# RWKV state stage: GroupNorm passes moved to ScalarE, zero blocks left out, and the block inverse computed in 64x64 quadrants

## What is computed

```python
def step(state, inp):
    rt, wt, kt, vt, kkt, at = inp
    sa = jnp.einsum('bhvk,bhk->bhv', state, -kkt)
    state = (state * wt[:, :, None, :]
             + sa[..., :, None] * (kkt * at)[..., None, :]
             + vt[..., :, None] * kt[..., None, :])
    yt = jnp.einsum('bhvk,bhk->bhv', state, rt)
    return state, yt
...
_, y = lax.scan(step, s0, xs)
...
mean = jnp.mean(y, axis=-1, keepdims=True)
var = jnp.mean(jnp.square(y - mean), axis=-1, keepdims=True)
y = ((y - mean) * lax.rsqrt(var + GN_EPS)).reshape(B, S, D_RWKV)
y = y * gn_g.astype(jnp.float32) + gn_b.astype(jnp.float32)
bonus = jnp.sum((r_h * k_h * r_k).astype(jnp.float32), axis=-1, keepdims=True) * v_h.astype(jnp.float32)
y = y + bonus.reshape(B, S, D_RWKV)
```

## Time and profile before

| | |
|---|---|
| median of 3 runs | 4568.9 us (4567.1 to 4570.67) |
| profiled execution | 4565.9 us, span of its instructions 4563.8 us |
| instructions | 68323 |
| mean granted clock of TensorE | 0.963 |
| TensorE busy | 4174.7 us, 91% of the span |
| VectorE busy | 2632.5 us, 58% |
| ScalarE busy | 1344.7 us, 29% |
| GpSimd busy | 633.4 us, 14% |

### The profile page before, as it was taken

One profiled execution on the slowest core, in us unless ns is written; L12 is line 12 of the kernel. 1 busy time (PEld: TensorE's weight loads), 2 busy tenths in 40 slices (PEclk: granted clock), 3 DMA queues, 4 the chain that ended last, 5 costly groups with the idle time before them and its releaser, 6 DMA issues. The chain is left out here.

```text
span 4563.8 us, 68323 instructions
## 1 busy us (share of the span) xinstructions
PE 4174.7 (91%) x24935; PEld 3522.7 (77%) x24992; DVE 2632.5 (58%) x5109; ACT 1344.7 (29%) x2721; POOL 633.4 (14%) x585
## 2 busy tenths in 40 slices
PE   9999799999799978999979996999989899899889
PEld 7888678887577758899978885778778677677667
DVE  5444444444566766888863345788743443677743
ACT  4323322222322221222221114666621211323221
POOL 0000011122000002333321110000000111122200
PEclk9999899999899988999989997999999999999989
DMA  3111311111444431111132325210034323423333
GB/s 147 49 64 64 130 62 63 62 62 55 168 135 140 140 123 53 50 48 48 49 115 110 115 101 172 77 35 20 10 139 164 129 103 135 135 90 98 99 132 115
DMA packets 218707, 434.13 MB, mean 95 GB/s; under 512 B 36819, under 2 KB 90836, under 8 KB 218422
## 3 DMA queue, kind: packets, MB, share of 16 engines
q1 hardware_dynamic: 218550, 432.09, 27.7%
HBM read 248.40 MB, written 146.93 MB: 87 GB/s over the span
## 5 line engine op out<-in xcount | busy, mean ns | idle before, releaser
L265 PE MATMUL rp_pj<-rp_w_high,rp_hT_high 128*128 128x512 f32 (+1 forms) x640 | 236.3, 378 | 22.7 <-DVE rp_gate L1429 17.8
L2569 DVE TENSOR_SCALAR_CACHE_REDUCE fa_sm<-fa_sc 128x512 f32<-128x512 f32 (+2 forms) x320 | 194.5, 610 | 92.6 <-PE fa_sc L2410 81.9
L265 PE MATMUL fp_pj<-fp_w_high,fp_hT_high 128*128 128x512 f32 (+2 forms) x640 | 216.5, 353 | 22.3 <-DMA fp_hT_low<-kept_low_dram 18.9
L266 PE MATMUL rp_pj<-rp_w_low,rp_hT_high 128*128 128x512 f32 (+1 forms) x640 | 231.5, 371 | 0.0
L266 PE MATMUL fp_pj<-fp_ahead_w_low,fp_hT_high 128*128 128x512 f32 (+2 forms) x640 | 214.5, 349 | 0.0
L265 PE MATMUL hg_pj<-hg_w_high,hg_hT_high 128*128 128x512 f32 x512 | 208.0, 406 | 4.6 <-DVE hg_w_low L255 4.6
L2424 PE MATMUL fa_tp<-fa_ident,fa_sm 128*128 128x128 f32 x1088 | 176.1, 283 | 33.1 <-DVE fa_pT_low L201 15.7
L2517 ACT CAST fa_pT_high<-fa_tp 128x512 fp32r<-128x512 f32 (+1 forms) x288 | 161.1, 560 | 148.5 <-PE fa_tp L2424 146.2
L265 PE MATMUL rc_pj<-rc_w_high,rc_hT_high 128*128 128x512 f32 (+1 forms) x512 | 190.1, 379 | 15.7 <-DMA rc_ident<-const_ident 10.1
L266 PE MATMUL hg_pj<-hg_w_low,hg_hT_high 128*128 128x512 f32 x512 | 201.5, 393 | 0.0
L201 DVE TENSOR_TENSOR fa_pT_low<-fa_tp,fa_pT_high 128x512 fp32r<-128x512 f32 (+1 forms) x288 | 189.0, 657 | 15.0 <-ACT fa_pT_high L2517 15.0
(11 more groups left out here) (571 smaller groups left out, 11185.0 us busy)
## 6 DMA issues: line engine op xcount, KB each, us to landing
rw_given<-rw_packed_dram SPq DMA_DIRECT2D x48, 512.0 KB, 3.9
rc_back<-rc_XB SPq DMA_DIRECT2D x48, 336.0 KB
rw_packed_dram<-rp_M SPq DMA_DIRECT2D x48, 256.0 KB, 2.6
rp_M<-rp_U SPq DMA_DIRECT2D x16, 728.0 KB, 4.7
hg_xt<-in_x SPq DMA_DIRECT2D x16, 512.0 KB, 3.7
kept_x_high_dram<-hg_hT_high SPq DMA_DIRECT2D x16, 512.0 KB, 3.5
kept_x_low_dram<-hg_hT_low SPq DMA_DIRECT2D x16, 512.0 KB, 4.3
sw_hT_high<-kept_x_high_dram SPq DMA_DIRECT2D x16, 512.0 KB, 3.7
```

The source lines that it names most:

```text
L265: pe.matmul(out, hT.high[:, kc, :], high[:, kc, lo:hi], start=kc == 0, stop=False)
L266: pe.matmul(out, hT.high[:, kc, :], low[:, kc, lo:hi], start=False, stop=False)
L2569: dve.tensor_scalar(sm[:, to:to + cols], bank_of(slot)[:, 0:cols], 0.0, NEG, ALU.add, ALU.max, accum_out=tops[:, four, c:c + 1]).then_inc( ...
```

## The change

- `multiply`, `spread`, `solve` stay. The four filler products go. The last step's increment of the state, which nobody reads, goes.
- `compact_blocks` waits for both halves of the products, masks 32x32 squares on 32 partitions each out of four banks taken as one tensor (`low_banks`), and adds two halves (two operations) instead of one reduce over 1024 elements.
- `invert_blocks` expands into `XQ`, 64 columns per head: the two diagonal quadrants side by side.
- `turn_first` and levels 4 and 5 run as 64x64 products, one for each diagonal quadrant; `X`, `T1` and `CT` shrink to 64 columns per head. `turn_first` becomes a product with `ident` instead of a transpose. The top level uses `BA`'s corner directly, 64x64, and VectorE writes its result negated into `XT`. ScalarE copies the quadrants of `XQ` to `XT`.
- The corners are cut by ScalarE with six copies of blocks (`corners`) into a matrix that is zeroed once; GpSimd's six products go and the constant `blocks` too.
- The two multiplications of the state by decays become one, with the product of the two factors (`renewal`), at the renewal.
- Of the normalisation, VectorE keeps the sum, the variance's scaling, the gate and the addition. ScalarE squares with a bias and an accumulator (8 operations, `square`) and scales with a shift and a factor (8 operations, `scale_y`).
- GpSimd's products for gate and rest wait for `parts_ready` and for `S_in`.
- b and k are loaded as soon as the increment is taken; v, the gate and the small rows after `rest_ready`.
- Values that TensorE waits for are put into registers ahead (`held`), with a wait on constants, always met, behind them.

```diff
-        X = sb("X", [P, RW_HEADS, P])
+        X = sb("X", [P, RW_HEADS, HALF])
+        XQ = sb("XQ", [P, RW_HEADS, HALF])
...
+            counters = [pe.alloc_register(f"rw_counter{n}") for n in range(3)]
+
+            def held(n, value):
+
+                if isinstance(value, int):
+                    return value
+                pe.reg_add(counters[n], value, 0)
+                return counters[n]
+
             def turn_first(i, pi, g):
...
-                    last = pe.transpose(B[2 * g][:, h * P:(h + 1) * P], XT[pi][:, 4 * g + h, :], ident[:])
+                    for q in quadrants:
+                        last = pe.matmul(B[2 * g][q, h * HALF:(h + 1) * HALF], XQ[q, 4 * g + h, :], ident[q, q], start=True, stop=True)
...
                 if stage == 0:
-                    pe.wait_ge(CT_ready, done + g + 1)
-                    pe.wait_ge(X_ready, done + g + 1)
-                    width = P // 2 if top else P
+                    turn, corner = held(0, done + g + 1), None if top else held(1, 2 * i + l - FIRST + 1)
+                    pe.wait_ge(consts_in, 16 * CONSTS)
+                    if not top:
+                        pe.wait_ge(CT_ready, corner)
+                    pe.wait_ge(X_ready, turn)
                     for h in hs:
-                        last = pe.matmul(B[2 * g][:, (h % 4) * P:(h % 4) * P + width], CT[:, h, :], X[:, h, 0:width], start=True, stop=True)
+                        cols = slice((h % 4) * HALF, (h % 4 + 1) * HALF)
+                        if top:
+                            last = pe.matmul(B[2 * g][HALF:P, cols], BA[pi][0:HALF, h, 0, HALF:P], X[0:HALF, h, :], start=True, stop=True)
+                        else:
+                            for q in quadrants:
+                                last = pe.matmul(B[2 * g][q, cols], CT[l - FIRST][q, h, :], X[q, h, :], start=True, stop=True)
...
+                    else:
+                        for h in hs:
+                            cols = slice((h % 4) * W, (h % 4 + 1) * W)
+                            for q in quadrants:
+                                pe.matmul(B[2 * g + 1][q, cols], XQ[q, h, :], halves_of(T1[q, h, :], l, 0), start=True, stop=True)
+                        for h in hs:
+                            cols = slice((4 + h % 4) * W, (4 + h % 4 + 1) * W)
+                            for q in quadrants:
+                                last = pe.matmul(B[2 * g + 1][q, cols], T1[q, h, :], halves_of(XQ[q, h, :], l, 1), start=True, stop=True)
...
-                    for n in range(4 if m else 0):
-                        pe.matmul(B[SPREAD[0]][:], pick_row[:, n, :], pick_row[:, 4:8, :].rearrange("p n t -> p (n t)"), start=True, stop=True)
                     spread(i, 0)
...
+            def corners(i, pi):
+
+                act.wait_ge(masked, 8 * i + 4)
+                for l in range(FIRST, LEVELS - 1):
+                    w = 1 << l
+                    for at in range(0, P, 2 * w):
+                        col = at % HALF + w
+                        one = act.copy(CT[l - FIRST][at:at + w, :, col:col + w], BA[pi][at:at + w, :, 0, at + w:at + 2 * w])
+                    one.then_inc(CT_ready, 1)
+
+            def square(t, pt, some):
+                act.wait_ge(neg_ready, t + 1)
+                for h in some:
+                    cols = slice(h * RW_DIM, (h + 1) * RW_DIM)
+                    one = act.activation(spare[:, cols], y[pt][:, cols], ACT.Square, bias=negmean[:, h:h + 1], accum_out=squares[:, h:h + 1])
+                one.then_inc(squared, 1)
+
+            def scale_y(u, pu):
+
+                act.wait_ge(rstd_ready, u + 1)
+                for h in range(RW_HEADS):
+                    cols = slice(h * RW_DIM, (h + 1) * RW_DIM)
+                    one = act.activation(y[pu][:, cols], y[pu][:, cols], ACT.Identity, bias=shift[:, h:h + 1], scale=rstd[:, h:h + 1])
+                one.then_inc(y_scaled, 1)
+
...
                 if m:
+                    if not (isinstance(t, int) and t == 0):
+                        scale_y(t - 1, 1 - pt)
                     act.wait_ge(Z_done, t + 1)
                     act.activation(Z[:], B[Z_BANK][:], ACT.Copy, scale=-1.0).then_inc(Z_ready, 1)
+                if pr:
+                    corners(i, pi)
...
+                        if l == LEVELS - 1:
+                            act.wait_ge(XT_ready, PER_TILE * i + 2 * (l - FIRST))
+                            act.copy(XT[pi][0:HALF, :, 0:HALF], XQ[0:HALF])
+                            act.copy(XT[pi][HALF:P, :, HALF:P], XQ[HALF:P]).then_inc(XT_copied, 1)
                         if follows and l < FIRST + 2:
                             take_two(i + 1, 1 - pi, l - FIRST)
+                        if m and l < FIRST + 2:
+                            square(t, pt, range(4 * (l - FIRST), 4 * (l - FIRST) + 4))
...
+                dve.wait_ge(products, 4 * i + 2)
+                for q in range(0, P, 2 * SMALL):
+                    own = slice(q, q + 2 * SMALL)
+                    tt(own32[own], low_banks[own, :].rearrange("p (s c) -> p s c", s=RW_HEADS)[:, :, own], again(near[own, own], RW_HEADS), ALU.mult)
+                dve.drain()
+                by_bank = own32[:].rearrange("p (r o k) c -> p o r k c", r=2, o=2)
+                by_head = Uc[:].rearrange("p (r k o) t -> p o r k t", r=2, k=2)
+                for o in range(2):
+                    tt(by_head[:, o], by_bank[:, o, :, :, 0:SMALL], by_bank[:, o, :, :, SMALL:], ALU.add)
...
+                tt(renewal[:], e_tot[pt][:, :, 1], e_tot[pi][:, :, 0], ALU.mult)
                 dve.wait_ge(inc_done, t + 1)
-                tt(heads(inc[:], PAIRS), heads(B[INC_BANK][:], PAIRS), again(own_head[:], PAIRS), ALU.mult)
+                tt(heads(inc[:], PAIRS), heads(B[INC_BANK][:], PAIRS), again(own_head[:], PAIRS), ALU.mult).then_inc(inc_taken, 1)
                 dve.drain()
                 tt(S[:], S[:], heads(inc[:], PAIRS), ALU.add)
                 dve.drain()
-                decay(pt, 1).then_inc(inc_taken, 1)
...
+                tt(S[:], S[:], spread(renewal[:], P), ALU.mult).then_inc(S_in, 1)
```

More of the change, by code:

```diff
@@ L1452, in rwkv @@
         given_of = lambda p, n: given[p][:, AT[n]:AT[n] + RW]
-        mean, var, rstd = (sb(n, [P, RW_HEADS]) for n in ("mean", "var", "rstd"))
+        negmean, squares, var, rstd, shift = (sb(n, [P, RW_HEADS]) for n in ("negmean", "squares", "var", "rstd", "shift"))
+        renewal = sb("renewal", [P, PAIRS])
         krT = [sb(f"krT{p}", [P, PAIRS, 2, P]) for p in range(2)]
@@ L1471, in rwkv @@
         out = [sb(f"out{p}", [P, RW]) for p in range(2)]
-        B = [s.bank(f"b{n}") for n in range(8)]
+        low_banks = ctx.enter_context(nc.psum_tensor("rw_b", [P, 4 * BANK], F32))
+        B = [*(low_banks[:, n * BANK:(n + 1) * BANK] for n in range(4)), *(s.bank(f"b{n}") for n in range(4, 8))]
         Z_BANK, Y_BANK, INC_BANK = 4, 5, 1
@@ L1530, in step @@
                         sp.wait_ge(inc_taken, t + 1)
+                    load_bk(later, 1 - pi)
+                    if t is not None:
                         sp.wait_ge(rest_ready, t + 1)
@@ L1647, in read_out @@
                 last.then_inc(y_done, 1)
-                for p in range(PAIRS):
-                    cols = slice(p * P, (p + 1) * P)
-                    last = pe.matmul(B[INC_BANK][:, cols], given_of(pt, "b")[:, cols], SA[:, cols], start=False, stop=p == PAIRS - 1)
-                last.then_inc(inc_done, 1)
+                if i is not None:
+                    for p in range(PAIRS):
+                        cols = slice(p * P, (p + 1) * P)
+                        last = pe.matmul(B[INC_BANK][:, cols], given_of(pt, "b")[:, cols], SA[:, cols], start=False, stop=p == PAIRS - 1)
+                    last.then_inc(inc_done, 1)
             def step(i, hi, pi, t, ht, pt):
@@ L1724, in step @@
                         act.wait_ge(first_turned, 2 * i + g + 1)
[L1725 removed]
+                        act.copy(X[:, 4 * g:4 * g + 4, :], heads(B[2 * g][:, 0:4 * HALF], 4)).then_inc(X_ready, 1)
                     for l in range(FIRST, LEVELS):
@@ L1738, in _ @@
             pool.memset(power[:], -0.5)
+            for one in (*CT, *XT):
+                pool.memset(one[:], 0.0)
             pool.drain()
@@ L1788, in tt @@
                 return dve.tensor_tensor(out_, a_, b_, op)
-            def decay(p, half):
-                return tt(S[:], S[:], spread(e_tot[p][:, :, half], P), ALU.mult)
             def mask_products(i, pi, n, r):
@@ L3464, in constants @@
     m["causal2"] = np.stack([s < t, s <= t], 1)
-    m["blocks"] = np.stack([((s >> (n + 1)) == (t >> (n + 1))) & ((s >> n) % 2 == 0) & ((t >> n) % 2 == 1) for n in range(LEVELS)], 1)
     m["own_block"] = s // SMALL == np.arange(SMALLS)[None]
```

172 lines of the change are left out of this document (81 added, 91 removed).

## The result

The changed kernel takes 4543.4 us (median of 5 runs, 4540.2 to 4552.4), the kernel before beside it 4567.1 (4566.5 to 4570.7). The ratio is 0.9949, 95% interval 0.9938 to 0.9960: faster, by 24 us where 52 were forecast. The profiled execution took 4543.4 us around a span of 4541.4.

What follows compares the result with a forecast made beforehand. TensorE (443 of 462 us busy) and VectorE (392) were both taken as nearly full. 15 x (4.7 - 1.7) plus 6.5 at the ends gave 52 us less than the 4568.9 median: 4517 us, range 4487 to 4560.

Steps and rivals of the forecast that it cites:

- The pairs: TensorE's turning and levels: two 64x64 products in diagonal quadrants run at once, 0.06 us a pair, 0.95 us for 16 pairs.
- The squarings: ScalarE, eight per step with an accumulator: 0.34 us each (bounds 0.21 and 0.50), four queued ahead of each T1 copy.
- the two stalls: TensorE idle 1.6 us before the second stage of level 5 and again before that of the top level, awaiting ScalarE.
- The start of the turning: Turning of the first blocks on TensorE begins 18.6 us after the start of the step's products.
- the step at the full clock: One step of the rwkv stage, without clock falls, takes 33.4 us against 38.1 before: 4.7 us less.
- the clock: TensorE's granted clock falls to 1.2 GHz once per step, costing 1.7 us (0 to 3.4).
- 15 x (4.7 - 1.7): Gain over 15 steps: 4.7 us shorter each, less 1.7 us each for one fall of TensorE's clock.
- Fillers: Removing TensorE's four filler products ahead of the spreading gains 0.9 to 1.0 us per step, on the path.
- (a): The forecast itself: pairs overlap and the clock falls at most once or twice a step, 4492 to 4543 us; chance 0.68.
- (b): Pairs of 64x64 products on TensorE do not overlap: step about 37.2 us, whole 4549 us; chance 0.13.
- (c): Clock falls at level 5's first wait, staying low until the next step's dense products: step 40.3, whole 4595 us; chance 0.09.
- (d): VectorE's relief is hidden and ScalarE's new work eats the rest: step 37.5 us, whole 4553 us; chance 0.10.

Runs made afterwards that it cites:

- the version without falls: Changed kernel with six throwaway products in each of TensorE's two waits and TensorE's loop written out step by step: 4499.6 us, ratio 0.9848.
- The written-out kernel: Changed kernel with TensorE's loop over two steps replaced by the 15 steps one after another, other engines keeping their loops: 4535.1 us, ratio 0.9927.
- the longer loops of the experiments: Kernel before with 60 or 120 small unused products added per step, giving 1564 or 1804 records in TensorE's loop: 4857.7 and 5054.8 us.
- the fastest version: Changed kernel with ScalarE's squarings moved behind the T1 copies and TensorE's loop written out: 4459.6 us, ratio 0.9763.

## Why the prediction was half right

**What held.** The bound and the sign. The pairs: priced at 0.95 a stage, 32 instructions lie 1.2 apart from start to start with the handover. The squarings: 0.34 forecast, 0.33 measured, and the two stalls at the two places named, 1.41 for 1.6. The start of the turning, 18.6 forecast, is 18.65 in the version without falls. VectorE was never late for level 5: the prediction had its line release that level, at 23.7, and its last update does end 5.1 us after the start of the turning as forecast, but TensorE's own transposes end at 5.4. The scalings took 0.34 each instead of 0.2, and the corners 2.06 in all instead of 1.8, both hidden.

**The sum, term by term**, for the 14 steps from the second on. In the kernel before they take 533.1 us, forecast was 14 x 35.1 = 491, measured 521.4. The 30 us between:

- the loop's branch, a term that was missing: 14.9 us of idle time less the 5 x 0.51 that a step's start has anyway, 12.4;
- the step at the full clock, forecast 33.4: the undisturbed version with fillers has 34.17, less the 0.1 by which these lengthen each wait 33.95. 14 x 0.55 = 7.7. It is spread over the chain behind the turning: of its nine pieces seven take 0.02 to 0.14 us more than forecast, most at the copies of `X` and at VectorE's last write;
- the clock: 521.4 - 12.4 - 14 x 33.95 = 33.7, which is 2.4 us per step where I took 1.7 (0 to 3.4). 14 x 0.7 = 9.9. The written-out kernel gives the same by itself: 36.34 - 33.95 = 2.4. One fall per step was right, 14 in these 14 steps, but eight of them lasted 6.8 us, one 13.7 and one 17.1, where the one that gave the price lasted 3.3.

The first step gave 4.5 instead of 6.0, and the last with the rest of the span 6.6 instead of 3.5.

So the step that failed is the sum "15 x (4.7 - 1.7)": it has 3.0 us of gain per step where 0.8 was measured over these 14. The clock's term lay in its range, at the dear side; the step of 33.4 had no range and was 0.55 too short; and the largest term, the branch, was not in the sum. The prediction listed the doubling of TensorE's instructions ("Instructions double") and priced only how fast they run, not where they are kept: the loop went from 1324 to 1806 records, and the branch from 0.21 to 3.3 us and more. The trace of before has the branch at 0.21 us and could not show where that ends; only the longer loops of the experiments did. But it could have been named as a cost with an unknown bound.

**Fillers.** "Gain 0.9 to 1.0, on the path" was too much: 0.62 in the fastest version, nothing in the kernel before.

**Rivals.** (a) held as a mechanism. That the time lies just at the slow end of its range is part chance, since 12 us of it are the branch, which (a) did not have. (b), that pairs don't overlap, is refuted by 1.15 us for 16 pairs and by the run with the quadrants apart; the rule of the Trainium skill ("TensorEngine Tiling (Array Packing)", Gotcha 1) behind it does not hold for diagonal quadrants here, and the measurement decides. That 4549 is near the time measured is chance. Its own sum also has a slip: with TensorE's work by its prices, 1.0 for the fillers, 0.9 lost at the turning, 0.2 at the two levels and 0.95 gained at the top, the work falls by 0.85 us per step and not by 1.9; the step of 37.2 goes with the 0.9. (c), that the clock stays low, is wrong: it lost 2.4 us per step, not the 5.1 from which that rival decides, though one fall lasted 17 us. (d) is wrong: the relief wasn't hidden, and ScalarE's extra work cost only what (a) had.

**Left open.** What ends a stretch at 1.2 GHz: a short one lasted 3.4 us, the one of 27 us above had TensorE busy for 25, and the longest 44, and no run tells why. So the branch's worth of 8, 36 and 81 us is measured but can't be worked out from the stalls. The falls of the clock in the changed kernel are put down to the two waits because filling both leaves none once the loop is written out; no run fills one of the two alone.

## What to carry to other kernels

When a change multiplies the instructions of an engine inside a loop, count them, and look at the duration of the loop's branch in the trace of before: here all jumps were fast with 1324 records, one of five slow with 1564 and all slow with 1804, and writing the loop out, or keeping it shorter, removed the stall. A short wait of TensorE is to be priced with the clock that it costs, and that is done most surely by putting throwaway products into it: if the kernel gets faster, the clock was the cost, and work queued ahead of the releasing copy on another engine is the place to mend. If it gets slower, nothing is decided while another stall is left: the same fillers cost 37 us with the loop and gained 35 without it. With squarings behind the copies and TensorE written out the change is worth 110 us instead of 24.

## What the hardware showed beyond that

- A gap of 0.65 to 0.99 us per step, nothing else, was enough to cost 29 us over the kernel before; its trace has three falls of the clock of 14 to 17 us, each behind a gap of 0.98 or 0.99. Four products of 512 columns in the gap prevented them at no cost.
- Filling two waits and leaving a third stall made the kernel slower than filling none (4580.6 against 4543.4).
- Two diagonal 64x64 products that write the same accumulator bank run at once, 0.06 us for a pair of instructions in the second stages (8 pairs from 1850.18 to 1850.64); issued eight instructions by eight instead, a first stage needs a third longer (1.54 for 1.15 us).
